# Values of two cycles multiplied together, first memory loads inside the last gate visit, sums of the last head shared with GpSimd

## The chip, the cores and the metric

The kernel runs on one core of a Trainium2 chip. The metric is the device time of one execution in microseconds, the median of several runs. Matrix products run on TensorE (PE; its weight loads are listed as PEld), the other engines are VectorE (DVE), ScalarE (ACT) and GpSimd (POOL); SyncE (SP) issues the DMAs. The times "granted clock 1.0" and "0.5" stand for TensorE at 2.4 and at 1.2 GHz.

## The reference: what is computed

One step of a hybrid encoder layer on 2048 prompt positions and 8 x 16 sample positions, width 1024. One input projection gives queries, keys, values, gates and state inputs. Three mixers run side by side and an output projection joins them:

```python
    fq, fk, fv, fg, ff, su, sg, mq, mg = split_columns(h @ w_in)
    fox_out = fox_attend(fq, fk, fv, logf).reshape(B, T, FOX_WIDTH) * jax.nn.silu(fg)
    ssm_out = ssm_y * jax.nn.silu(sg)
    mem_out = memory_attention(mq, mem_k, mem_v).reshape(B, T, MEM_WIDTH) * jax.nn.silu(mg)
    mix = jnp.concatenate([fox_out, ssm_out, mem_out], axis=-1) @ w_out
    return x + mix, fk, fv, logf, h_re, h_im
```

The forgetting attention (fox) has 8 heads of 64 channels, causal; the memory attention (mem) has 4 heads of 64 over 256 memory tokens. Both take the softmax of their scores over the keys and multiply it with the values.

## The kernel before

The kernel has three stages. The input projections run until about 789 us: 7 passes (state, keys, values, queries, memkv, memq, gate), each over the 17 position tiles (memkv over its two memory tiles), a tile being a "visit" of three parts. Attention of the prompt runs from there to about 1262 us, and the output projection to the end at 1453 us. All three are written as lists of steps; each engine walks the same list and does the steps that are its own, so the list is each engine's order, and semaphores hold the engines together.

**The attention list** (`attention_order`, L1924). Each of the 8 heads has six units of four query tiles: fox0, fox4, mem0, mem4, fox8, fox12 (fox8 is the fox unit whose first tile is 8). A unit has one "scores" block for each key tile: 4, 8, 2, 2, 12 and 16, which makes 44 a head, 352 in all. Four blocks make a cycle: 11 cycles a head, 88 in all (`CYCLE = 4`). Cycles are counted from 0 here. In one cycle stand, in this order:

- "copied": ACT takes the outputs of the units that ended in the cycle before out of PSUM (L2621)
- "scores": PE, two matmuls a block, L2481 and L2486 (and a mask, L2483); "exp": ACT, L2610, into one of 16 slots of `probs_turned`
- "top": PE makes scores in the other orientation some 20 blocks ahead (L2464, L2468, mask L2471), and DVE takes the maximum of each row (L2812, L2818). With the last top of a unit DVE writes `diag` (L2829)
- "row": PE turns a unit's `diag` into a row (L2475) and ACT copies it next to the queries (L2600). The second matmul of a unit's first score waits for that copy
- "add": the exponentials of a block are added to the unit's sum, on POOL, but blocks 2, 3, 6 and 10 of fox8 and fox12 on DVE; of the last head (head 7) all blocks of fox8 and fox12 on DVE (L2780, L2782). "both" (DVE, L2838) joins the two sums; it waits for POOL's part
- "den": two cycles after a unit has ended PE turns its sum (L2494) and DVE adds it up (L2844) and inverts it (L2848)
- "values": PE multiplies exponentials and values (L2512), two tiles of 64 output columns side by side
- in head 7 from its second cycle on: "w_split" (ACT, L2628) and "w_low" (POOL, L2735) split two rows blocks of the output weights, "t_split" (ACT, L2640) and "t_low_early" (POOL, L2739) split sums of them, "gated" (POOL, L2706) multiplies the sample tile by its gates. "mix" (PE, L2535) turns that tile and needs "gated". The pair list ends with the first products of the output projection ("product", PE, L2580), "first_sum" and "y" (DVE, L2892, L2929)

**The PSUM ring** (`Ring`): scores, tops, rows and dens take six banks in turn. PE may fill a bank when the step that used it before has been read: a score by ACT's exp, a top or a den by DVE, a row by ACT.

**The seam between the stages.** The first 12 tops and row 0 are three "hooks" ("attention" steps 0 to 2), laid after the three parts of the last gate visit (`beside[NV - 1, n]`, L373). The steps "first" (DVE L1561) and "second" (DVE L1587, then SP's store L735) of a visit finish a tile's gates; those of the last visit stand behind the visit. Two things wait for them: the sixth bank of the ring, and the first "values". The loads of head 0's values and memory keys (`load_values(sp, 0)`, 8 DMAs, L2242) stand at the start of SP's attention program, and so behind the store of the last gate tile. The tops 12 to 15 (mem0, mem4; L2464), in the first cycle, wait for these loads.

## Time and profile before

| | us |
|---|---|
| median of 3 runs | 1453.31 (1453.03 to 1454.95) |
| profiled execution | 1454.54 |
| its span | 1452.8 |
| busy: PE / DVE / ACT / POOL | 1397.1 / 976.3 / 610.5 / 553.5 |

The span is the time between the first and the last instruction of the trace; 1.7 us lie around it. PE is busy for 96% of it, so the profile is read from PE: first how long it stood and for whom, then at which clock it ran, then what lies between its matmuls. Busy sums count overlapping matmuls once, and a matmul's own length (0.40 us) is longer than the distance at which such matmuls start (0.24 us).

### The profile page before, as it was taken

The page shows a single profiled execution, that of the slowest core. Times are in us where ns is not written, and L with a number is a line of the kernel's source. Part 1 is how long each engine was busy: PE and PEld are TensorE (multiplying, and loading weights), DVE is VectorE, ACT ScalarE, POOL GpSimd, SP SyncE. Part 2 cuts the span into 40 slices and gives each one's busy share as a digit, 9 for nine tenths or more (in the row PEclk, how much of TensorE's full clock was granted, in tenths as well). Part 3 has the DMA queues.
Part 4 walks back from the last instruction along what each step waited for, and adds up shares of the span by engine and source line. Part 5 has one row for each costly group of instructions (what it writes and reads, how often), then busy time and mean ns, then how long its engine had stood idle before and what let it go on. Part 6 is the DMA issues. An engine that isn't in the chain of part 4 may idle for free.

```text
span 1452.8 us, 24958 instructions
## 1 busy us (share of the span) xinstructions
PE 1397.1 (96%) x8510; PEld 1105.9 (76%) x8510; DVE 976.3 (67%) x1827; ACT 610.5 (42%) x1220; POOL 553.5 (38%) x580
## 2 busy tenths in 40 slices
PE   8999999999999989999998899999999999899998
PEld 8999767788877767777776677777777777578886
DVE  4789754782566787655334577787786767987774
ACT  6766422432434363435332344444444445431221
POOL 1121433100043252112003366776776658534442
PEclk9999999999999999999999899999999999899999
DMA  7884799986279587788983935726627432446552
GB/s 226 305 285 174 249 235 254 317 258 193 84 181 350 162 263 254 256 276 275 329 274 103 259 74 113 149 49 128 133 51 153 93 62 66 140 161 200 185 186 89
DMA packets 207565, 275.82 MB, mean 190 GB/s; under 512 B 49424, under 2 KB 146096, under 8 KB 203952
## 3 DMA queue, kind: packets, MB, share of 16 engines
q1 hardware_dynamic: 206400, 274.22, 64.9%
q8 instruction: 70, 1.15, 0.3%
q14 instruction: 55, 0.45, 0.1%
q10 hardware_dynamic: 1040, 0.00, 0.0%
HBM read 186.93 MB, written 86.00 MB: 188 GB/s over the span
## 4 chain that ended last, share of the span: by engine, by line
PE 55%; DVE 7%; issue 3%; DMA 2%; SPq 2%; ACT 2%; POOL 1%; DVEq 0%; ACTq 0%; POOLq 0%
PE in_g L925 13%; PE attn_pv L2512 8%; PE attn_s L2580 6%; PE attn_s L2481 5%; PE attn_pv L2580 5%; PE attn_s L2486 4%; PE attn_s L2468 4%; DVE attn_acc_v L2782 2%; DVE attn_tops L2818 2%; PE in_b L1100 1%; DMA in_xu<-scratch_xt 1%; DVE attn_den L2844 1%; POOL in_hv L1808 1%; PE attn_s L2475 1%; PE attn_s L2494 1%
## 5 line engine op out<-in xcount | busy, mean ns | idle before, releaser
L925 PE MATMUL in_g<-in_wh,in_xh 128*128 128x512 f32 (+2 forms) x904 | 331.4, 380 | 5.4 <-DVE in_wl L1519 1.9
L925 PE MATMUL in_g<-in_wl,in_xh 128*128 128x512 f32 (+2 forms) x904 | 321.9, 369 | 0.0
L925 PE MATMUL in_g<-in_wh,in_xl 128*128 128x512 f32 (+2 forms) x904 | 235.0, 379 | 1.4 <-DVE in_xl L1530 1.3
L2782 POOL TENSOR_TENSOR attn_probs<-attn_probs,attn_probs_turned 128x512 f32<-128x512 f32 (+3 forms) x184 | 196.4, 1067 | 86.9 <-ACT attn_probs_turned L2610 65.6
L2610 ACT ACTIVATE attn_probs_turned<-attn_s 128x512 f32<-128x512 f32 (+1 forms) x352 | 161.5, 544 | 155.9 <-PE attn_s L2486 155.9
L2818 DVE TENSOR_REDUCE attn_tops<-attn_s 128x1 f32<-128x512 f32 (+3 forms) x288 | 159.7, 617 | 94.0 <-PE attn_s L2468 71.5
L925 PEld LDWEIGHTS in_g<-in_wh,in_xh 128*128 128x128 f32 x904 | 165.5, 189 | 39.7 <-issue 6.3
L925 PEld LDWEIGHTS in_g<-in_wl,in_xh 128*128 128x128 f32 x904 | 165.6, 189 | 28.0
L925 PEld LDWEIGHTS in_g<-in_wh,in_xl 128*128 128x128 f32 x904 | 158.0, 189 | 34.8 <-issue 5.2
L1806 POOL TENSOR_SCALAR in_hs<-in_hs 128x8 f32<-128x8 f32 (+1 forms) x53 | 19.7, 372 | 401.8 <-DVE in_hs L1557 401.8
L2512 PE MATMUL attn_pv<-attn_probs_turned,attn_v 128*64 128x256 f32 (+1 forms) x1216 | 146.3, 371 | 0.0
L2512 PEld LDWEIGHTS attn_pv<-attn_probs_turned,attn_v 128*64 128x64 f32 x1216 | 86.9, 140 | 48.4 <-issue 20.2
L1217 ACT ACTIVATE in_xh<-in_xu 128x512 fp32r<-128x512 f32 x174 | 99.6, 623 | 49.0 <-DMA in_xu<-scratch_xt 49.0
L1530 DVE TENSOR_TENSOR in_xl<-in_xu,in_xh 128x512 fp32r<-128x512 f32 x106 | 68.7, 689 | 32.8 <-ACT in_xh L1217 32.3
L1808 POOL TENSOR_TENSOR in_hv<-in_hs,all_neghalf 128x8 f32<-128x8 f32 (+1 forms) x53 | 84.0, 1585 | 4.4
L2780 POOL TENSOR_TENSOR attn_probs<-attn_probs_turned 128x512 f32<-128x512 f32 x38 | 50.3, 1332 | 59.0 <-ACT attn_probs_turned L2610 59.0
L1258 ACT ACTIVATE in_x_turned<-in_tr 128x512 fp32r<-128x512 f32 (+1 forms) x53 | 27.5, 520 | 88.8 <-PE in_tr L947 79.9
L2481 PE MATMUL attn_s<-all_x,all_y 128*128 128x512 f32 (+3 forms) x160 | 62.3, 390 | 1.9 <-DVE in_stage L1587 1.9
L2481 PE MATMUL attn_s<-attn_qa,attn_ka 128*128 128x512 f32 (+3 forms) x160 | 62.2, 389 | 1.7 <-DVE attn_den L2844 1.7
L2486 PE MATMUL attn_s<-all_x,all_y 97*128 97x512 f32 (+3 forms) x160 | 61.3, 383 | 0.5 <-ACT all_x L2600 0.5
L2486 PE MATMUL attn_s<-attn_qb,attn_kb 97*128 97x512 f32 (+3 forms) x160 | 61.2, 383 | 0.0
L1577 DVE TENSOR_TENSOR in_work<-in_g,in_hr 128x512 f32<-128x512 f32 (+1 forms) x53 | 31.4, 592 | 37.9 <-POOL in_hr L1811 37.0
(380 smaller groups left out, 2756.2 us busy)
## 6 DMA issues: line engine op xcount, KB each, us to landing
in_xu<-scratch_xt SPq DMA_DIRECT2D x87, 512.0 KB, 5.3
in_xl<-scratch_xt SPq DMA_DIRECT2D x34, 512.0 KB, 4.5
in_raw<-in_w_in SPq DMA_DIRECT2D x40, 256.0 KB, 5.4
scratch_xt<-in_xu SPq DMA_DIRECT2D x19, 512.0 KB, 4.5
scratch_xt<-in_xl SPq DMA_DIRECT2D x17, 512.0 KB, 5.0
scratch_k<-in_x_turned SPq DMA_DIRECT2D x17, 512.0 KB, 7.2
scratch_q<-in_x_turned SPq DMA_DIRECT2D x17, 512.0 KB, 5.4
in_x_turned<-in_x_prompt SPq DMA_DIRECT2D x16, 512.0 KB, 4.9
```

Source lines behind the costliest of these rows:

```text
L925: last = X.matmul(g_ps[b][:, 0:m], x, ws[:, c, w0:w0 + m], start=(c == 0 and h == 0 and ws is wh), stop=(c == KC - 1 and h == 1))
L1217: F(xh[:, item_visit[j] % 2, 4 * h:4 * h + 4, :], xu[:, j % 2, 4 * h:4 * h + 4, :], ACT.Copy)\
L1530: V.tensor_tensor(xl[:, v % 3, 4 * h:4 * h + 4, :], xu[:, j % 2, 4 * h:4 * h + 4, :], fl(xh[:, v % 2, 4 * h:4 * h + 4, :]), ALU.subtract). ...
L1808: G.tensor_tensor(hv[:, 0:m], hs[:, 0:m], K.neghalf[:, 0:m], ALU.pow).then_inc(s_hchain, 1)
L2468: last = X.matmul(bank[:, at:at + n, :], qb[h][0:LANE, q], kb[h][0:LANE, keys], start=True, stop=not masked)
L2481: X.matmul(bank[:, part:, :], y2[h][:, keys], x2[h][:, q], start=True, stop=False)
L2486: X.matmul(bank[:, part:, :], y1[h][0:FULL, keys], x1[h][0:FULL, q], start=False, stop=True)\
L2512: last = X.matmul(v_ps[u.n % 2][lane * HD:(lane + 1) * HD, tiles[0] // 2:EACH // 2, :], vals[:, k, :], pt[:, s % SLOTS, tiles[0]::2, :], s ...
L2580: last = X.matmul(y_ps[at], ms[left][:, c, :], ws, start=(begins and c == 0 and k == 0), stop=(ends and c == HALF - 1 and k == 2))
L2610: F(pt[:, s % SLOTS, at:, :], ring_ps[ring.at["scores", s]][:, at:, :], ACT.Exp).then_inc(s_exp, 1)
L2782: E.tensor_tensor(acc[:, part:, :], acc[:, part:, :], mine, ALU.add).then_inc(added[engine], 1)
L2818: V.tensor_reduce(top_parts[:, joined[u.n] % 2, i, k // 4:k // 4 + 1], bank[:, 0:n, :].rearrange("p n k -> p (n k)"), AX.X, ALU.max).then_ ...
```

## The change

1. `TOGETHER = 2`: the "values" of an even and the following odd cycle now stand together at the end of the odd one, sorted by unit, each unit's "copied" right behind its last values. "den" steps stand in odd cycles only, ahead of the values, for units that ended two or more cycles earlier.
2. `load_values(sp, 0)` and the waits ahead of it move out of SP's attention program into `sync_begin`, which SP runs at hook 0.
3. The hooks move by one part: hook 0 after part 1, hook 1 after part 2, hook 2 (with row 0) behind "first" and "second" of the last visit.
4. In head 7 fox8's sums are shared as in other heads: 4 blocks on DVE, 8 on POOL, and a "both". fox12's stay on DVE.
5. "t_split" and "t_low_early" 0 and 1 stand one cycle earlier, ahead of "gated" 0. Product (0, 1) stands ahead of the last "den".

```diff
-    for n in range(HOOKS):
-        beside[NV - 1, n] = [("attention", n)]
-    order = projection_order(items, visits, behind, beside)
+    for n in range(HOOKS - 1):
+        beside[NV - 1, n + 1] = [("attention", n)]
+    order = projection_order(items, visits, behind, beside) + [("attention", HOOKS - 1)]
...
+                if what == "attention" and n[0] == 0:
+                    K.begin[0](sp)
...
-            late = u.head == FOX_HEADS - 1 and u.first >= 8
+            late = u.head == FOX_HEADS - 1 and u.blocks > 12
...
-        if c - 1 in ended:
-            order += [("copied", u) for u in ended[c - 1]]
...
-        if c - 2 in ended:
-            order += [("den", u) for u in ended[c - 2]]
-        order += [("values", b) for b in mine]
         ended[c] = [n for n in range(len(units)) if CYCLE * c < score_end[n + 1] <= CYCLE * (c + 1)]
         order += [("both", n) for n in ended[c]]
+        waiting += mine
+        if c % TOGETHER == TOGETHER - 1 or c == cycles - 1:
+            order += [("den", n) for e in range(c) if e + 2 <= c for n in ended[e] if ("den", n) not in order]
+            for n in sorted({scores[b][0].n for b in waiting}):
+                order += [("values", b) for b in waiting if scores[b][0].n == n]
+                if score_end[n + 1] <= waiting[-1] + 1:
+                    order.append(("copied", n))
+            waiting = []
...
+        if n in (KC, KC + 1):
+            order += [("t_split", n - KC), ("t_low_early", n - KC)]
         if n == KC + 1:
             order.append(("gated", 0))
-        if n in (KC + 1, KC + 2):
-            order += [("t_split", n - KC - 1), ("t_low_early", n - KC - 1)]
...
-    order += [("copied", n) for n in ended[cycles - 1]]
-    order += [("product", 0, 0)] + [("den", n) for n in ended[cycles - 1]]
-    order += [("product", 0, 1), ("first_sum", 0), ("t_split", 2), ("t_split", 3), ("mix", 1)]
+    order += [("product", 0, 0), ("product", 0, 1)] + [("den", n) for n in ended[cycles - 1]]
+    order += [("first_sum", 0), ("t_split", 2), ("t_split", 3), ("mix", 1)]
...
-        def sync_program(sp):
+        def sync_begin(sp):
             sp.wait_ge(K.s_cleared, 1)
...
+        def sync_program(sp):
             sp.wait_ge(*K.end_products)
```

The order of SP at the seam, before (`in_stage` are gate tiles that are stored, `attn_v` to `attn_mv` the 8 loads):

```order
L861 DMA scratch_mwide<-in_late 64x128
L735 DMA scratch_fox_gate<-in_stage 128x512 x4
L2242 DMA attn_v<-out_fox_v_prompt 128x16x64
L2242 DMA attn_mqa<-scratch_mq 64x1024 x2
L2242 DMA attn_mqb<-scratch_mq 64x1024
```

And now:

```order
L863 DMA scratch_mwide<-in_late 64x128
L737 DMA scratch_fox_gate<-in_stage 128x512 x3
L2246 DMA attn_v<-out_fox_v_prompt 128x16x64
L2246 DMA attn_mqa<-scratch_mq 64x1024 x2
L2246 DMA attn_mqb<-scratch_mq 64x1024
L2246 DMA attn_mka<-scratch_mk 64x256 x2
L2246 DMA attn_mkb<-scratch_mk 64x256
L2246 DMA attn_mv<-out_mem_v_prompt 128x2x64
L737 DMA scratch_fox_gate<-in_stage 128x512
```

The 8 loads have passed the store of the last gate tile.

The order of PE where the first cycles meet, before (L2464 are the mem tops, L2475 row 1, L2512 the values of cycle 0, L2481 and L2486 the scores of cycle 1):

```order
L2464 MATMUL attn_s<-attn_mkb,attn_mqb 128x256 x8
L2468 MATMUL attn_s<-all_y,all_x 128x512 x2
L2475 MATMUL attn_s<-attn_diag,attn_onesr 128x512
L2512 MATMUL attn_pv<-attn_probs_turned,attn_v 64x256 x2
L2512 MATMUL attn_pv<-attn_probs_turned,attn_v 64x128
L2512 MATMUL attn_pv<-attn_probs_turned,attn_v 64x256
L2512 MATMUL attn_pv<-attn_probs_turned,attn_v 64x128 x3
L2481 MATMUL attn_s<-all_x,all_y 128x512
L2486 MATMUL attn_s<-all_x,all_y 128x512
```

And now, where the lines stand five further down (L2480 is row 1, L2486 and L2491 are the scores):

```order
L2469 MATMUL attn_s<-attn_mkb,attn_mqb 128x256 x8
L2473 MATMUL attn_s<-all_y,all_x 128x512 x2
L2480 MATMUL attn_s<-attn_diag,attn_onesr 128x512
L2486 MATMUL attn_s<-all_x,all_y 128x512
L2491 MATMUL attn_s<-all_x,all_y 128x512
```

The scores of cycle 1 stand directly behind row 1, and the values of both cycles behind the tops and rows of cycle 1.

The order of POOL in head 7 from its fifth cycle on, before (L2735 "w_low", L2706 "gated" 0, L2739 "t_low_early"):

```order
L2780 TENSOR_TENSOR attn_probs<-attn_probs_turned 128x512 x2
L2735 TENSOR_TENSOR attn_w_lo<-attn_w_raw,all_y 128x1024 x2
L2735 TENSOR_TENSOR attn_w_lo<-attn_w_raw,all_x 128x1024 x2
L2735 TENSOR_TENSOR attn_w_lo<-attn_w_raw,all_y 128x1024 x2
L2706 TENSOR_TENSOR attn_out<-attn_out 128x512
L2706 TENSOR_TENSOR attn_out<-attn_out 128x256
L2739 TENSOR_TENSOR attn_t_lo<-attn_t_raw,attn_t_hi 128x1024 x2
```

And now (L2785 and L2787 are adds, L2740 "w_low", L2744 "t_low_early", L2711 "gated" 0):

```order
L2785 TENSOR_TENSOR attn_probs<-attn_probs_turned 128x512
L2740 TENSOR_TENSOR attn_w_lo<-attn_w_raw,all_y 128x1024
L2787 TENSOR_TENSOR attn_probs<-attn_probs,attn_probs_turned 128x512 x3
L2740 TENSOR_TENSOR attn_w_lo<-attn_w_raw,all_x 128x1024
L2787 TENSOR_TENSOR attn_probs<-attn_probs,attn_probs_turned 128x512
L2787 TENSOR_TENSOR attn_probs<-attn_probs,attn_probs_turned 128x384
L2787 TENSOR_TENSOR attn_probs<-attn_probs,attn_probs_turned 128x128
L2740 TENSOR_TENSOR attn_w_lo<-attn_w_raw,all_x 128x1024
L2740 TENSOR_TENSOR attn_w_lo<-attn_w_raw,all_y 128x1024 x2
L2744 TENSOR_TENSOR attn_t_lo<-attn_t_raw,attn_t_hi 128x1024 x2
L2711 TENSOR_TENSOR attn_out<-attn_out 128x512
L2711 TENSOR_TENSOR attn_out<-attn_out 128x256
```

Seven adds have come in, and "gated" 0 stands behind both "t_low_early".

## Rows read from the trace of the kernel before

**Rows 1.** The page, busy time of TensorE: us, share of the span, instructions.
```profile
PE 1397.1 (96%) x8510; PEld 1105.9 (76%) x8510; DVE 976.3 (67%) x1827; ACT 610.5 (42%) x1220; POOL 553.5 (38%) x580
```
**Rows 2.** Busy us by stretch: PE, PEld, DVE, ACT, POOL, then granted clock, DMA.
```profile
804.80:811.80 7.00, 6.94 (x27) 5.23 (x28) 5.07 (x8) 0.97 (x2) 0.00 (x0) 0.50 1.01 207
...
812.00:1228.00 416.00, 413.88 (x2693) 310.60 (x2693) 307.24 (x537) 196.01 (x422) 280.41 (x245) 1.00 0.50 109
...
1269.00:1272.70 3.70, 3.70 (x12) 3.02 (x13) 2.06 (x4) 0.00 (x0) 0.30 (x1) 0.54 1.04 373
```
**Rows 3.** Who PE waited for from 740 us: total us, times, longest.
```profile
PE attn_s L2464 <- DMA attn_mv<-out_mem_v_prompt: 9.9, 1, 9.9
PE attn_s L2494 <- DVE attn_acc_v L2782: 3.5, 1, 3.5
PE attn_s L2468 <- DVE attn_den L2844: 3.3, 7, 2.1
...
PE attn_pv L2580 <- DVE attn_probs L2929: 1.7, 1, 1.7
```
**Rows 4.** Timeline at the seam: start us, us, engine, line, [idle before <- releaser].
```profile
794.53 0.39 SPq L2242 DMA_DIRECT2D attn_v<-out_fox_v_prompt  x1
...
781.90 0.75 DVE L1561 TENSOR_SCALAR in_work<-in_g,in_half 128x512 f32<-128x512 f32 x1 [4.09 <-ACT in_work L1240]
...
793.28 0.69 DVE L1587 SCALAR_TENSOR_TENSOR in_stage<-in_work 128x512 f32<-128x512 f32 x1
...
794.03 0.39 PE L2481 MATMUL attn_s<-all_x,all_y 128*128 128x256 f32 x1 [1.94 <-DVE in_stage L1587]
...
804.86 2.04 PE L2464 MATMUL attn_s<-attn_mkb,attn_mqb 66*128 66x256 f32 x8 [9.92 <-DMA attn_mv<-out_mem_v_prompt]
```
**Rows 5.** Timeline of PE around the values of one cycle, in short windows.
```profile
1000.69 0.49 PE L2494 MATMUL attn_s<-all_ident,attn_probs 128*128 128x128 f32 x3
...
1001.11 1.95 PE L2512 MATMUL attn_pv<-attn_probs_turned,attn_v 128*64 128x256 f32 x16
...
1001.81 0.60 PE L2512 MATMUL attn_pv<-attn_probs_turned,attn_v 128*64 128x256 f32 x4
...
1002.67 0.39 PE L2512 MATMUL attn_pv<-attn_probs_turned,attn_v 128*64 128x256 f32 x2
1002.99 0.50 PE L2481 MATMUL attn_s<-attn_qa,attn_ka 128*128 128x512 f32 x1
1003.32 0.40 PE L2486 MATMUL attn_s<-attn_qb,attn_kb 97*128 97x512 f32 x1
1003.56 0.40 PE L2481 MATMUL attn_s<-attn_qa,attn_ka 128*128 128x512 f32 x1
```
**Rows 6.** Timeline of DVE after the tops of that cycle, and of a row.
```profile
1005.41 2.48 DVE L2818 TENSOR_REDUCE attn_tops<-attn_s 128x1 f32<-128x512 f32 x4 [1.56 <-PE attn_s L2468]
...
1008.13 0.97 DVE L2829 TENSOR_TENSOR attn_diag<-all_ident,attn_negmax 128x512 fp32r<-128x512 f32 x1
...
1012.08 0.45 PE L2475 MATMUL attn_s<-attn_diag,attn_onesr 128*128 128x512 f32 x1
...
1012.56 0.59 ACT L2600 ACTIVATE attn_qb<-attn_s 1x512 fp32r<-1x512 f32 x1 [1.44 <-PE attn_s L2475]
```
**Rows 7.** Last head: POOL, DVE and PE by time, and POOL's adds as a group.
```profile
1225.82 4.75 POOL L2735 TENSOR_TENSOR attn_w_lo<-attn_w_raw,all_y 128x1024 fp32r<-128x1024 f32 x2
...
1250.26 2.89 POOL L2735 TENSOR_TENSOR attn_w_lo<-attn_w_raw,all_y 128x1024 fp32r<-128x1024 f32 x1 [1.52 <-ACT all_y L2628]
1253.11 2.86 POOL L2706 TENSOR_TENSOR attn_out<-attn_out 128x512 f32<-128x512 f32 x2
...
1246.36 10.15 DVE L2782 TENSOR_TENSOR attn_acc_v<-attn_acc_v,attn_probs_turned 128x512 f32<-128x512 f32 x6
...
1258.39 0.96 PE L2535 MATMUL attn_s<-all_ident,attn_out 128*128 128x128 f32 x6
...
L2782 POOL TENSOR_TENSOR attn_probs<-attn_probs,attn_probs_turned 128x512 f32<-128x512 f32 (+3 forms) x184 | 196.4, 1067 | 86.9 <-ACT attn_probs_turned L2610 65.6
```

6 lines of the change are left out of this document (3 added, 3 removed).

## The prediction

> **What bounds the kernel now.** I read the page first: TensorE is busy for 1397.1 of 1452.8 us [rows 1], so a gain must come from PE's standing, its clock, or what lies between its matmuls. The second view is who PE waited for. Behind the seam these waits are few and large: 9.9 us for the loads of head 0, 3.5 us for the last sum, 3.3 us for a den's reading (2.1 of it once), 1.7 us at a product [rows 3]. The third view, the busy time by stretch, shows that two of them cost twice: after the 9.9 us PE worked 7.0 us at a granted clock of 0.50, and after the 3.5 us 3.7 us at 0.54 [rows 2]. Between 812 and 1228 us PE is busy for 413.88 of 416 us, with DVE at 307 and POOL at 280 [rows 2]: only what lies between the matmuls is to be had there. Fourth, the timeline shows what does: the values and their neighbours [rows 5].
>
> **The seam (edits 2 and 3).** The first of the 8 loads was issued at 794.53, and the mem tops, which need all 8, started at 804.86: 10.3 us [rows 4]. What held the loads was the store of the last gate tile, whose data DVE finished at 793.28 + 0.69. SP now only has the store of the tile before ahead of them. Its DVE steps start at 781.90 with L1561 (0.75), then L1587 (0.69, as in the last tile), which no longer has hook 0 in between: 783.4. With the store's issue (0.39, as a load's) the loads start at about 783.8 and are there at 794.1. The other condition is DVE, which reads the twelve early tops and does the last tile's steps in another order but with the same work, and was done at 793.97. The last tile's two steps now stand ahead of hook 2's tops, so the wait of 1.94 us for them [rows 4] turns into a wait for those tops. I take 794.2 for the mem tops: 10.7 us earlier.
>
> In addition PE did 6.94 us of work at half the clock after its long wait [rows 2]; at full clock that is 3.5 us less. A wait of about 3 us remains ahead of 794, after which the clock may still be low, but then PE waits for DVE anyway. **Seam: -14.2 us**, bounds -9 (the loads land 2 us later and the clock stays low for the whole of PE's 7 us) and -16 (PE waits for nothing else behind them).
>
> **Switches between values and the rest (edit 1).** In [rows 5] pairs of value matmuls start 0.215 us apart (1001.81 to 1002.67, four pairs). A transpose has 128 columns where a pair has 256, so 0.11 us; the third of the row starts at 1000.69 + 0.22, and the values at 1001.11, 0.20 later where 0.11 is due: 0.09. From 1001.11 to 1001.81 three pairs take 0.70 for 0.645: 0.05. From the last pair to the scores 0.32 for 0.215: 0.10. Between the first two score matmuls 0.33 for 0.24: 0.09. Together 0.33 us for each visit to the values. There were 88, now there are 44. As a small edge stays where tops now meet scores, I take 0.30: 44 x 0.30 = **-13.2 us**, bounds -9 and -14.5.
>
> **What the values covered.** They lay between the tops of one cycle and the scores of the next, 1.88 us. Now an even cycle's tops are directly followed by scores, and four prices are due.
> (a) A row in an even cycle whose unit starts in the next. fox12's row stands one cycle ahead of its scores; for heads 0, 2, 4 and 6 that is an even cycle. From the row's matmul to the end of ACT's copy 1.07 us pass (1012.08 to 1012.56 + 0.59) [rows 6], of which PE fills 0.47 with the row and one score matmul: 0.65 us, four times, 2.6 us.
> (b) A row in an odd cycle whose last top was read in the even one. Counted from the pair's first score (1002.99), DVE starts on the tops at 2.4, ends at 4.9, and `diag` is there at 6.1 [rows 6]; PE reaches the row after 2 x 1.97 (scores) + 2 x 0.95 (tops) = 5.8. About 20 rows are of that kind: 0.15 each, 3 us; if adds are ahead of DVE, 0.5 each.
> (c) The first three pairs have 12, 10 and 10 tops. Twelve readings at 0.62 us (2.48 for four) [rows 6] and three `diag` are 10 us for DVE, in the stretch in which PE has 7.5 us of scores and tops: 2.5 us, and 1.5 us for the other two.
> (d) The fourth top of an even cycle is read at 4.9 and its bank wanted at 5.1. So DVE must be ready when tops come. Its work in a pair: 5.0 for tops, 0.9 for each add, both or den, 1.1 for a `diag`: 6 to 8 us, but 10.5 in the pairs with three dens, of the pair's 10.8. A late start of some tenths in these: 2 us in all; nothing at best, 12 at worst (0.3 in each pair).
> Sum of the waits: 2.6 + 3 + 4 + 2 = 11.6; **+11.6 us**, bounds +4 and +25.
>
> **The last head (edits 4 and 5).** DVE has 7 adds less and one "both" more there; from 1228 on it was never idle, and the waits of 2.1, 1.7 and 3.5 us for it should go. But POOL takes its place. It worked without a pause up to 1230.57 (1225.82 + 4.75) [rows 7], at "w_low" 3. From there now follow, ahead of "gated" 0: one pair add (1.3), 3 adds (3.4), w_low (2.4), 3 adds (2.6, two are narrow), 3 w_low (7.9), 2 t_low_early (5.3; nearest row: w_low 2.89, same width) and gated 2.86: 25.8 us, to 1256.4, by 1.07 us an add and 2.4 to 2.9 for a split. "mix" 0 stood at 1258.39 and needs it [rows 7]. PE, freed of its waits, would be there at about 1250, so it waits some 4 to 6 us for POOL, and the gain up to mix 0 is 2.0 us. Behind it PE has the values of two cycles (3.6) where it had one at a low clock (2.83): product 0 starts 1.6 us earlier than before. On from there, product (0, 1) covers the last sum (2.8 of the 3.5 us), but "first_sum" now comes after it, and product (0, 2) waits 1.8 us for that (den 0.9, two sums 1.4). The product that waited 1.7 us waits for a chain of DVE steps behind the same den, which begins 3 us earlier: 4.6 us gained in all. Half clocks after the two new waits give back about 2.7. 1.6 + 4.6 - 2.7: **-3.5 us**, bounds -11 (POOL keeps up) and +4 (DVE and POOL hold each other).
>
> Here a rule of the Trainium skill speaks against edit 4. First the row: six adds of DVE took 10.15 us while POOL ran [rows 7], 1.69 each. The rule ("SBUF — State Buffer", section "Who interferes with whom"): a DVE instruction with two SBUF inputs and a GpSimd one that reads SBUF exclude each other, and the later blocks for the whole instruction. My sum has 1.0 us an add for the 15 adds of fox12; by the rule POOL is never idle beside them now, and they take what the row shows.
>
> **Sum.** -14.2 - 13.2 + 11.6 - 3.5 = -19.3 us on the profiled execution's 1454.5: 1435.2. The median of the runs lies 1.2 us below that execution: 1434.0 us.
>
> **The rivals.**
> - *The cover was not needed* (chance 0.20). DVE was busy for 307 of 416 us [rows 2], POOL less; if (b), (c) and (d) cost 4 us instead of 9, and POOL reaches "gated" in time, 5 + 6 more is gained: 1423. Against it: readings come in bursts.
> - *DVE's adds at 1.69 us* (0.13). 15 x 0.69 = 10.4 us more for DVE behind the last both; it has some 6 us in hand before PE wants the last sum. The last den comes 4 us later: 1438. The rule above is this mechanism. Against it: POOL's 12 steps there can each hold up one add at most, and some will meet DVE's other steps.
> - *Half the gain is lost in bursts* (0.16). The waits are 25 instead of 11.6: 1447. For it: (d), since a late DVE shifts both top groups of a pair.
> - *Nothing gained* (0.04): 1451 to 1456, if also the loads run slower beside the last gate products.
> - *Slower* (0.05). DVE misses the second top group in every pair: its adds now stand between two top groups 2.95 us apart, of which the reading takes 2.5. The gains outside are 30.9 us, so it decides from 0.70 us a pair on; at 1.0 us, 44 us are lost: 1467. Against it: the bank of the first top is wanted 0.8 us after it is read, and the values of a pair (3.6 us) let DVE catch up each time.
>
> **How the numbers follow.** The forecast at 1434 has 0.42. Left out are the slower case, "nothing gained" and the outer half of the first and third rival: the range is 1421 to 1448. A measurement of this kernel tells 0.2% (2.9 us) from no change: faster 0.91, within 0.04, slower 0.05.
>
> **What would show it.** Right: the 9.9 us wait is gone and the mem tops start near 794; 44 groups of values of 3.6 us; the clock at 1.0 from about 800 on; PE's waits in the middle are many and under 0.7 us, for ACT's row copy and DVE's `diag` and tops; a wait of 3 to 6 us at mix 0 for POOL's gated; product (0, 2) waits for first_sum. Wrong: waits over 1 us in most pairs, or a clock at 0.5 in the middle, or values that start no closer to each other than before.

## The result: slower, where a gain of 19 us was forecast

| | median us | from, to | runs |
|---|---|---|---|
| before | 1454.13 | 1453.03, 1455.73 | 4 |
| changed | 1460.82 | 1459.53, 1461.62 | 4 |

The ratio is 1.0045, with a 95% interval of 1.0029 to 1.0060. The forecast was 1434.0 us, with a range of 1421 to 1448. Of all runs below one is left out of its comparison, a run of before_den_first of 1937.7 us at a mean granted clock of 0.66. The profiled execution of the changed kernel took 1461.6 us, its span is 1459.9 us, 7.1 more than before. TensorE's busy time is 2.7 us more, so most of the 7.1 are standing:

```profile
PE 1399.8 (96%) x8510; PEld 1120.1 (77%) x8510; DVE 980.8 (67%) x1820; ACT 611.0 (42%) x1220; POOL 569.2 (39%) x587
```

The second view is the busy time by stretch, in the columns of [rows 2]. The stretches are cut at the same pieces of work in both kernels: start of the mem tops, first scores of cycle 2, first scores of cycle 78, first product matmul, its 61st matmul. First the kernel before:

```profile
804.90:817.10 12.20, 12.20 (x59) 8.75 (x59) 8.17 (x14) 4.11 (x8) 3.58 (x3) 0.72 1.02 213
817.10:1208.30 391.20, 389.08 (x2537) 292.09 (x2535) 291.94 (x509) 178.88 (x387) 259.31 (x230) 1.00 0.50 109
...
1208.30:1262.40 54.10, 50.03 (x306) 35.38 (x305) 44.63 (x61) 33.58 (x68) 36.00 (x21) 0.94 0.25 68
1262.40:1285.50 23.10, 17.89 (x76) 13.81 (x76) 16.82 (x22) 5.03 (x9) 8.23 (x7) 0.93 0.71 235
```

and then the changed kernel:

```profile
793.40:808.00 14.60, 14.35 (x60) 10.63 (x60) 8.56 (x15) 4.79 (x10) 6.70 (x6) 0.58 1.03 209
...
808.00:1212.10 404.10, 389.57 (x2536) 302.11 (x2535) 300.87 (x509) 179.61 (x387) 265.47 (x230) 0.98 0.47 103
...
1212.10:1274.50 62.40, 51.34 (x306) 37.64 (x305) 44.26 (x57) 33.17 (x68) 48.63 (x31) 0.89 0.33 94
1274.50:1292.50 18.00, 16.13 (x77) 12.84 (x77) 10.33 (x17) 5.04 (x8) 3.49 (x4) 1.00 0.63 208
```

The changed kernel is 9.1 us ahead when cycle 2 starts, loses 12.9 from there to cycle 78 (the "middle" below), loses 8.3 to the first product, gains 5.1 behind it, and is level after that: -9.1 + 12.9 + 8.3 - 5.1 = +7.0.

**The seam** went as drawn up to the mem tops. In the timeline of the changed kernel (SP, then PE) the first load is issued at 783.06 and the mem tops start at 793.40, 11.5 us earlier than in [rows 4]:

```profile
783.06 0.39 SPq L2246 DMA_DIRECT2D attn_v<-out_fox_v_prompt  x1
...
793.40 2.02 PE L2469 MATMUL attn_s<-attn_mkb,attn_mqb 66*128 66x256 f32 x8
...
797.37 0.79 PE L2491 MATMUL attn_s<-all_x,all_y 97*128 97x512 f32 x1 [0.25 <-ACT all_x L2605]
```

But the granted clock was 0.50, its lower level of 1.2 GHz, from 792.0 to 805.7, so 12.3 us of what follows the mem tops ran at half speed, where before it was 7.0 [rows 2]. In the kernel before the clock was low for longer, from 794.6 to 811.8, but PE stood for all but 0.34 of the first 10.2 us of it; now work runs in that time. From the mem tops to cycle 2 the changed kernel takes 2.4 us more.

**The waits of PE** from 808 to 1212 us, whom it waited for, total, times and longest:

```profile
PE attn_s L2480 <- DVE attn_diag L2834: 4.0, 8, 0.9
PE attn_s L2473 <- DVE attn_den L2849: 3.3, 4, 1.1
PE attn_s L2499 <- DVE attn_negmax L2817: 2.7, 3, 0.9
PE attn_s L2486 <- DVE attn_negmax L2817: 1.9, 3, 0.6
PE attn_s L2491 <- ACT all_x L2605: 1.8, 4, 0.4
PE attn_s L2473 <- DVE attn_tops L2823: 0.8, 1, 0.8
```

They sum to 14.5 us; before it was 2.0 in the same stretch (1.1 and 0.9 for denominators' banks). L2480 is the row, L2473 the tops, L2499 the transposes of a denominator, L2486 and L2491 the scores. **And the clock fell** four times in the middle, where before it never did. Two of the four, each with the stretch ahead of it:

```profile
891.00:897.80 6.80, 5.66 (x40) 3.82 (x37) 6.59 (x9) 2.45 (x5) 6.64 (x5) 1.00 0.01 2
897.80:901.20 3.40, 3.40 (x10) 2.72 (x10) 2.02 (x5) 1.62 (x3) 1.05 (x2) 0.50 0.41 154
...
966.00:972.90 6.90, 5.83 (x42) 4.32 (x39) 6.79 (x12) 1.86 (x5) 6.28 (x5) 1.00 0.29 69
972.90:979.70 6.80, 6.80 (x32) 5.38 (x33) 3.77 (x6) 2.38 (x6) 4.19 (x6) 0.50 1.04 211
```

PE had stood for 1.1 us of the stretch ahead of each of these two falls, for 1.1 of the 10.5 us ahead of the third, and for 0.7 of the 7.0 us ahead of the fourth. That does not tell when the clock falls, though. Here is another stretch of the same kernel, which ends with a wait of 1.08 us for a denominator's bank at 1090.19; the clock behind it stayed at 1.00:

```profile
1083.00:1090.20 7.20, 6.12 (x50) 4.17 (x48) 7.10 (x10) 1.98 (x5) 6.63 (x5) 1.00 0.03 8
```

The four low stretches (897.8, 972.9, 1010.5 and 1147.0) are 17.0 us long, and half of that, 8.5 us, is lost. The middle then reads: waits +12.5, clock +8.5, and -8.1 that is left over: +12.9. The -8.1 is a remainder, taken here for what the switches saved; no run measures it by itself.

One of these waits, in the timeline of PE and of DVE around 971 us:

```profile
969.72 0.45 PE L2473 MATMUL attn_s<-attn_kb,attn_qb 66*128 66x512 f32 x1
971.24 0.56 PE L2473 MATMUL attn_s<-attn_kb,attn_qb 66*128 66x512 f32 x2 [1.07 <-DVE attn_den L2849]
...
968.20 0.69 DVE L2834 TENSOR_TENSOR attn_diag<-all_ident,attn_negmax 128x512 fp32r<-128x512 f32 x1
968.80 1.78 DVE L2787 TENSOR_TENSOR attn_acc_v<-attn_acc_v,attn_probs_turned 128x512 f32<-128x512 f32 x1
970.51 0.68 DVE L2849 TENSOR_REDUCE attn_den<-attn_s 128x4 f32<-128x512 f32 x1
```

The second top block wants the bank that holds the transposed sums of a denominator. The reduction that empties it takes 0.68 us, but stands on DVE behind an addition, and that addition takes 1.78 us where it takes 0.69 alone.

**The last head.** PE waits 3.85 us ahead of the first of the last twelve score blocks, runs at half clock behind that, and then waits 5.11 us for GpSimd's gate (PE, then DVE, then POOL):

```profile
1250.00 0.79 PE L2486 MATMUL attn_s<-attn_qa,attn_ka 128*128 128x512 f32 x1 [3.85 <-DVE attn_den L2849]
...
1267.89 1.54 PE L2540 MATMUL attn_s<-all_ident,attn_out 128*128 128x128 f32 x6 [5.11 <-POOL attn_out L2711]
...
1246.52 2.82 DVE L2843 TENSOR_TENSOR attn_acc_v<-attn_acc_v,attn_probs 128x512 f32<-128x512 f32 x1 [2.93 <-POOL attn_probs L2787]
1249.26 0.68 DVE L2849 TENSOR_REDUCE attn_den<-attn_s 128x4 f32<-128x512 f32 x1
1249.97 0.18 DVE L2853 RECIPROCAL attn_rmem<-attn_den 128x4 f32<-128x4 f32 x1
...
1252.21 6.65 DVE L2787 TENSOR_TENSOR attn_acc_v<-attn_acc_v,attn_probs_turned 128x512 f32<-128x512 f32 x6
...
1255.52 2.79 POOL L2740 TENSOR_TENSOR attn_w_lo<-attn_w_raw,all_y 128x1024 fp32r<-128x1024 f32 x1 [3.96 <-ACT all_y L2633]
...
1262.82 2.66 POOL L2744 TENSOR_TENSOR attn_t_lo<-attn_t_raw,attn_t_hi 128x1024 fp32r<-128x1024 f32 x1 [1.68 <-ACT attn_t_hi L2645]
1265.44 2.39 POOL L2711 TENSOR_TENSOR attn_out<-attn_out 128x512 f32<-128x512 f32 x2
```

The denominator whose bank is wanted at 1250.00 is a memory unit's (its inverse goes to `attn_rmem`). Its reduction stood on DVE behind the new "both" of fox8 (L2843), and that waited 2.93 us for GpSimd's part of the sum and then took 2.82 us itself. So this wait comes of edits 1 and 4 together: in merge_only and in tail_only, which have one of them each, and in after_den_first, where the reduction stands ahead of the "both", no such wait is in the traces. The three waits for DVE that stood here before (2.1, 1.7 and 3.5 us [rows 3]) are all gone.

### The profile page after: what moved, and what is told of

It reads as the page before. It is cut to its first block, busy times and chain, and to the rows that moved or that the text cites. A ratio compares the mean times of both kernels' runs of the same rounds, so it can differ in the third digit from the quotient of the medians.

```text
span 1459.9 us, 24959 instructions
## 1 busy us (share of the span) xinstructions
PE 1399.8 (96%) x8510; PEld 1120.1 (77%) x8510; DVE 980.8 (67%) x1820; ACT 611.0 (42%) x1220; POOL 569.2 (39%) x587
## 4 chain that ended last, share of the span: by engine, by line
PE 53%; DVE 6%; issue 5%; POOL 3%; ACT 2%; DMA 2%; SPq 1%; DVEq 0%; ACTq 0%; POOLq 0%
PE in_g L927 13%; PE attn_pv L2517 9%; PE attn_s L2585 6%; PE attn_pv L2585 5%; PE attn_s L2486 4%; PE attn_s L2491 4%; PE attn_s L2473 4%; DVE attn_tops L2823 1%; PE in_b L1102 1%; PE attn_s L2499 1%; DMA in_xu<-scratch_xt 1%; POOL in_hv L1810 1%; DVE attn_negmax L2817 1%; POOL attn_probs L2787 1%; PE attn_s L2480 1%
## 5 line engine op out<-in xcount | busy, mean ns | idle before, releaser
L2787 POOL TENSOR_TENSOR attn_probs<-attn_probs,attn_probs_turned 128x512 f32<-128x512 f32 (+3 forms) x190 | 213.1, 1122 | 97.7 <-ACT attn_probs_turned L2615 74.5
L2517 PE MATMUL attn_pv<-attn_probs_turned,attn_v 128*64 128x256 f32 (+1 forms) x1216 | 141.1, 375 | 0.0
L2517 PEld LDWEIGHTS attn_pv<-attn_probs_turned,attn_v 128*64 128x64 f32 x1216 | 93.0, 143 | 43.4 <-issue 13.8
L2486 PE MATMUL attn_s<-attn_qa,attn_ka 128*128 128x512 f32 (+3 forms) x160 | 62.8, 392 | 5.8 <-DVE attn_den L2849 3.9
L2785 POOL TENSOR_TENSOR attn_probs<-attn_probs_turned 128x512 f32<-128x512 f32 x39 | 50.1, 1294 | 45.1 <-ACT attn_probs_turned L2615 44.9
L2491 PE MATMUL attn_s<-all_x,all_y 97*128 97x512 f32 (+3 forms) x160 | 63.0, 394 | 2.0 <-ACT all_x L2605 2.0
L2491 PE MATMUL attn_s<-attn_qb,attn_kb 97*128 97x512 f32 (+3 forms) x160 | 63.4, 396 | 0.0
L2486 PE MATMUL attn_s<-all_x,all_y 128*128 128x512 f32 (+3 forms) x160 | 61.9, 387 | 1.5 <-DVE attn_tops L2823 1.5
```

Of the source, the lines that this page charges most:

```text
L2486: X.matmul(bank[:, part:, :], y2[h][:, keys], x2[h][:, q], start=True, stop=False)
L2491: X.matmul(bank[:, part:, :], y1[h][0:FULL, keys], x1[h][0:FULL, q], start=False, stop=True)\
L2517: last = X.matmul(v_ps[u.n % 2][lane * HD:(lane + 1) * HD, tiles[0] // 2:EACH // 2, :], vals[:, k, :], pt[:, s % SLOTS, tiles[0]::2, :], s ...
L2787: E.tensor_tensor(acc[:, part:, :], acc[:, part:, :], mine, ALU.add).then_inc(added[engine], 1)
```

## Experiments: each part alone

Four kernels: the merging alone (edit 1), the seam alone (2 and 3), the last head alone (4 and 5), and all but the merging.

```
merge_only          CYCLE, TOGETHER = 4, 2;   seam and last head as before
seam_only           CYCLE, TOGETHER = 4, 1;   last head as before
tail_only           CYCLE, TOGETHER = 4, 1;   seam as before
seam_tail_no_merge  CYCLE, TOGETHER = 4, 1
```

Expected of merge_only:

> The kernel before with edit 1 alone: the values of two cycles together, the seam and the last head as they were. Theory A (the new short waits of TensorE behind tops, rows and dens cost their own length and also take its clock down): between the scores of cycle 2 and those of cycle 78 some 390 us become 400 to 406, with about 15 us of waits where there were 2, four or five stretches of 3.4 us at the low clock where there was none, and 10 to 11 us saved between values and scores; in all 5 to 14 us slower than before. Theory B (the low clock in the middle comes from another edit, such as the changed seam, and the waits alone are paid for by the saved switches): the clock stays at 1.0 between cycle 2 and 78, and the kernel is within 5 us of before.

Of seam_only:

> The kernel before with edits 2 and 3 alone (the loads of head 0 issued at hook 0, the hooks one part later). Both theories: the mem tops start near 793.4 instead of 804.9, PE works the first 13 us of attention at half clock as in the changed kernel, and 7 to 11 us are gained, all of them before the scores of cycle 2; the middle stays as before, without low clock.

Of tail_only:

> The kernel before with edits 4 and 5 alone (fox8 of the last head shared with GpSimd, both early splits ahead of gated 0, product (0, 1) ahead of the last den). Theory A: GpSimd becomes the late one, mix 0 waits for gated 0 by 3 to 6 us, and the last head with the first products is between 3 us faster and 4 us slower than before. Rival (the late gated 0 in the changed kernel came from the merged values, not from these edits): no wait at mix 0 over 1 us, and 5 to 10 us gained.

Of seam_tail_no_merge:

> The changed kernel with the values of each cycle on their own again (edits 2 to 5 without edit 1). Theory A: the sum of the two runs that change the seam and the last head alone, so some 5 to 14 us faster than before; the middle between cycle 2 and 78 as before (391 us). Theory B: about as slow as the changed kernel, or slower.

| kernel | median us | ratio to before, 95% interval | start of cycle 2 against before | middle, us | from cycle 78 on, against before |
|---|---|---|---|---|---|
| before | | | 0 | 391.2 | 0 |
| changed | 1460.8 | 1.0045 (1.0029 to 1.0060) | -9.1 | 404.1 | +3.3 |
| merge_only | 1467.8 | 1.0101 (1.0075 to 1.0128) | -1.8 | 399.4 | +3.7 |
| seam_only | 1448.0 | 0.9961 (0.9948 to 0.9973) | -9.0 | 391.1 | +4.6 |
| tail_only | 1459.8 | 1.0041 (1.0025 to 1.0056) | -3.2 | 391.1 | +6.5 |
| seam_tail_no_merge | 1451.3 | 0.9988 (0.9975 to 1.0000) | -8.1 | 391.2 | +5.3 |

The last three columns are from one profiled execution each. The start of cycle 2 differs between kernels without the seam edit too (0 to -3.2 here, and up to +1.9 in the kernels of the next section), so two or three microseconds in that column, and what follows from it in the whole, is nothing. The middle does not: in all kernels without merging and with DVE's order as before it is 391.1 to 391.2. The rows of merge_only's and seam_only's middle:

```profile
815.30:1214.70 399.40, 383.73 (x2535) 298.32 (x2534) 300.72 (x509) 179.38 (x387) 265.49 (x230) 1.00 0.47 105
```
```profile
808.10:1199.20 391.10, 389.00 (x2536) 292.09 (x2534) 291.89 (x509) 178.88 (x387) 259.57 (x230) 1.00 0.50 109
```

**What follows.** The seam is the only part that gains: 4.9 us, where 7 to 11 were expected, since 4.6 of the 9.0 us ahead are lost again behind cycle 78. Merging costs 14.8 us alone by the medians (10 in the profiled execution, the fastest of the four), where 5 to 14 were expected, and 9.5 beside the other edits (1460.8 against 1451.3). The edits on the last head cost 6.9 us alone, and there neither expectation held: PE did not wait at mix 0, and nothing was gained. Seam and last head together came out at -1.7 us, where -5 to -14 had been expected. In merge_only PE waited 15.7 us in the middle, in the changed kernel 14.5, but the clock fell there for 3.4 us and here for 17.0. Taken one by one from the two traces the waits are the same to 0.05 us, but for two more in merge_only (0.85 and 0.31 us). So the same waits cost 1.7 us more at the clock in one execution and 8.5 in the other. What decides it is not in the waits, and was not found.

## Experiments: what the merged cycles wait for

Two theories. **A**: DVE's additions stand ahead of what PE waits for. **B**: the order asks too soon, since a row follows its tops without values between them, and eight score and eight top blocks in a row must pass through six banks. merge_light leaves most of VectorE's additions out (its denominators of fox8 and fox12 are then not the reference's), before_light is its control, and merge_row_late gives the diagonal more time.

```
merge_light, before_light  (heads 0 to 6, DVE only)
-    E.tensor_tensor(acc[:, part:, :], acc[:, part:, :], mine, ALU.add)
+    E.tensor_tensor(acc[:, part:, 0:8], acc[:, part:, 0:8], mine[:, :, 0:8], ALU.add)
-    (a block's first sum)
+    E.memset(acc, 1.0)
merge_row_late
     order += [("values", b) ...]
+    while rows < len(units) and top_end[rows + 1] <= before:
+        order.append(("row", rows)); rows += 1       # was ahead of the additions
```

Expected of merge_light, before_light and merge_row_late:

> merge_only with most of VectorE's work on the sums of probabilities left out in heads 0 to 6: its first sum of a block is a memset of 1.0, and each later addition takes 8 of 128 columns, so the denominators of fox blocks 8 and 12 are not the reference's. All waits and the order stay. Theory A (the 15 us of new waits from 808 to 1212 us are VectorE being late: its additions stand ahead of the tops, diagonals and denominators that TensorE waits for, and 40 us of the additions lie in that stretch): those waits fall from about 15 us to under 5, and scores of cycle 2 to scores of cycle 78 take 391.2 - 10.6 = about 381 us instead of 399.5 (merge_only) and 391.2 (before); the whole kernel is some 15 us under merge_only, about 1452. Rival B (the waits come of the order itself: a row or a bank is asked for too soon after the score block that fills it, whatever VectorE has to do): the waits keep 10 us or more and the stretch takes 393 or more. Rival C (the clock): low stretches of the clock remain in the middle though the waits are gone.

> The kernel before with the same work of VectorE left out as in merge_light: the control. Before waits only 2.0 us in the stretch from the first cycles to cycle 78, so both theories expect it to take 389 to 391.2 us there; if it gains more, the lighter VectorE also gives something that has nothing to do with merged cycles (the gap between two kinds of block, contention), and this is to be taken off merge_light's gain. The last head keeps its additions, so the whole kernel should be at 1450 to 1454 us.

> merge_only with the row matmul of each unit written behind the eight value blocks of an odd cycle instead of ahead of them, so that VectorE has some 5 us more between the last tops and the row that needs their diagonal. Theory A (VectorE is late by 0.9 us at a time): the waits for the diagonal (5.8 us in 10) go, but VectorE's lateness shows at the next thing asked of it, the banks of tops and denominators and the score blocks that need the row's copy: the middle stretch gains 0 to 4 us of the 8.3. Rival B (the order asks too soon for the row): the middle gains the 5.8 us and the 2.5 us of the copies' waits, and comes to the 391.2 of before or under it.

The middle of merge_light, with its longest wait under it, of before_light, and of merge_row_late with its two longest waits:

```profile
816.80:1210.30 393.50, 382.22 (x2535) 298.13 (x2534) 282.58 (x509) 179.19 (x387) 257.80 (x230) 1.00 0.48 106
...
PE attn_s L2477 <- DVE attn_diag L2838: 5.0, 10, 0.9
```
```profile
814.30:1200.80 386.50, 386.50 (x2537) 291.33 (x2535) 272.57 (x509) 178.87 (x387) 252.80 (x231) 1.00 0.50 111
```
```profile
818.00:1222.30 404.30, 386.49 (x2535) 302.00 (x2533) 298.49 (x509) 181.08 (x389) 266.82 (x230) 0.98 0.47 103
...
PE attn_s L2470 <- DVE attn_den L2846: 6.8, 4, 2.5
PE attn_s L2483 <- DVE attn_den L2846: 4.3, 2, 2.2
```

Medians: 1461.5 us (ratio 1.0051, 1.0033 to 1.0068), 1449.8 (0.9971, 0.9958 to 0.9984), 1470.1 (1.0120, 1.0102 to 1.0139). **Neither theory alone holds.** With light additions merging costs 393.5 against 386.5, 7.0 us of the 8.2 that it costs with full ones, and 11.1 us of waits are left: A falls as the main cause, and the numbers of B came (10 us of waits or more, 393 us or more). With the rows late the diagonal's waits are gone, as B says, but 11.1 us for denominators' banks stand where 4.5 were, the clock fell for 13.6 us instead of 3.4, and the middle is 4.9 us longer: both expectations missed (0 to 4 us gained by A, the 391.2 of before by B). What the later row gives, VectorE's lateness and the clock take back, and more. The control was a miss of its own: 4.7 us gained where 2.2 at most were expected, with 2.0 us of waits in the profile to be had. That pointed at DVE's order.

The next two take both away, one by leaving work out, one with all work done. merge_adds_late holds the additions of an even cycle back until behind the tops and denominators of the odd one, so that DVE adds during the values.

```
merge_adds_late
-    order += [("add", b) for b in mine]              # each cycle, ahead of den
     if c % TOGETHER == TOGETHER - 1 or c == cycles - 1:
         order += [("den", n) ...]
+        order += [("add", b) ...] + [("both", n) ...]   # of both cycles
merge_row_late_light  =  merge_row_late + merge_light
merge_adds_row_late   =  merge_adds_late + merge_row_late
```

> Both measures at once: the rows behind the values of an odd cycle, and VectorE's additions of heads 0 to 6 left out as in merge_light (the fox denominators of blocks 8 and 12 are again not the reference's). Theory A+B (the new waits have two parts that cover each other: the diagonal is asked for too soon after its tops, and VectorE comes late to the banks of denominators): with both taken away the middle stretch (cycle 2 to cycle 78, 391.2 us before, 386.5 with the light VectorE alone) falls to 376 to 380 us, the 10.6 us of switches at last seen. Rival B (the six banks of the score ring: eight score and eight top blocks in a row ask for more than ScalarE and VectorE can empty, whatever stands in the order): waits for negmax, tops and denominators of 6 us or more stay, and the stretch takes 384 us or more.

> merge_only, with the additions of an even cycle held back on VectorE and GpSimd until after the tops and the denominators of the odd cycle, so that in the burst of scores and tops VectorE only empties banks, and adds while TensorE works through the eight value blocks. All work is done. If VectorE's additions in the burst are what makes it late (Theory A), the middle stretch falls from 399.5 us (merge_only) to about merge_light's 393.5 or under it; if it is the chain of four tops, their negmax and the diagonal (B), the waits for the diagonal (5.8 us) stay and it takes 396 or more. ScalarE's exponentials wait for additions 16 blocks back, so additions that come 4 blocks later can cost something too, at most 2 us.

> merge_only with additions and denominators in the order of merge_adds_late and the rows behind the value blocks as in merge_row_late; all work is done. merge_adds_late took 389.8 us from cycle 2 to cycle 78 (391.2 before, 387.1 unmerged with the denominators first) and still waited 7.1 us for diagonals; merge_row_late_light took 387.6 with most additions left out. Theory: the diagonals' waits go, and 387 to 389 us are left, no better than the unmerged kernel with the same VectorE order: merged cycles then give nothing, because what the switches save goes into waits for the six banks. Rival: 383 us or less, and merging pays after all once VectorE's order is right.

The middles, in that order:

```profile
819.00:1206.60 387.60, 379.42 (x2536) 297.38 (x2534) 280.18 (x509) 180.49 (x389) 258.69 (x230) 1.00 0.48 107
```
```profile
818.50:1208.30 389.80, 379.83 (x2535) 297.68 (x2534) 290.10 (x509) 179.40 (x387) 264.85 (x230) 1.00 0.49 107
```
```profile
815.60:1224.80 409.20, 393.83 (x2536) 307.66 (x2534) 290.29 (x509) 181.59 (x389) 264.51 (x230) 0.96 0.47 103
...
PE attn_s L2484 <- DVE attn_tops L2821: 8.8, 6, 2.1
```

Medians 1455.7 (1.0012, 1.0001 to 1.0023), 1457.2 (1.0023, 1.0014 to 1.0032) and 1477.8 (1.0173, 1.0148 to 1.0197). In merge_row_late_light (376 to 380 us expected, or 384 and more) 7.8 us of waits stay, 3.6 of them for the row's copy by ScalarE, and the middle is 1.1 us longer than before_light's: even then merging does not pay. merge_adds_late brings the middle to 389.8 with all work done, 9.6 us under merge_only's and better than expected (393.5), though 4.4 us of waits for diagonals stay (a later expectation names 7.1, which is not the middle's). It is the only merged kernel with all work done whose middle lies under that of the kernel before, by 1.4 us; in all it is 3.3 us slower than before, and in its last head PE waits 7.3 us for VectorE's sums. merge_adds_row_late was a miss on both sides: 387 to 389 or at most 383 had been expected, and it is the slowest of all. With rows late the score block behind a row wants a bank whose tops DVE has not read, up to 2.1 us, and the clock fell for 23.8 us (865.3, 981.4 and 1100.9). Why the two measures, each fair or bearable alone, do this together was not followed further.

## Experiments: the order on VectorE

The control and the 971 us timeline say the same: DVE reduces a denominator behind the additions of its cycle, and the bank is wanted before. One line moved, on DVE alone (PE has no additions):

```
+    order += [("den", n) ...]
     order += [("add", b) for b in mine]
     ...
-    order += [("den", n) ...]
```

> seam_only with one order changed on VectorE alone: the reduction of a denominator is written ahead of the four additions of its cycle instead of behind them. In the last head these additions take 1.7 to 2.3 us each instead of 0.69 because GpSimd works beside them, and the reduction of block 8's denominator stands behind four of them, with the last score block waiting for its bank 4.1 us. Theory: that wait goes, and of the 4.5 us that the tail of seam_only gave back, 2 to 4 return: 1444 to 1446 us. Rival: the sums of block 12 end later by as much, since VectorE waits for the transposes of the denominator, and the wait only moves to the products' bank or the fold (5.3 us now): no difference from 1448.

> The changed kernel with the same order on VectorE. In its middle 3.3 us of waits for the bank of a denominator and 4.4 us between transposes of denominators should shrink by half, in its last head the 3.9 us before the last score block go: 1453 to 1457 us where the changed kernel takes 1460.8. By the rival (what waits for VectorE is the engine's whole load, not the place of the reduction) it stays at 1459 to 1462.

> The kernel before, with the reduction of a denominator ahead of its cycle's additions on VectorE, and nothing else changed. The middle stretch should fall by the 4.0 us of seam_den_first (391.2 to 387.2), because the time between top blocks falls from 15.5 to 10.8 us in all; in the last head the wait of the last score block (1.7 us) and of the tops (2.1 us) should go, so that the whole kernel takes 1446 to 1449 us. Rival (the gain needs the earlier seam as well): 1450 or more.

> A repeat of seam_den_first (1441.4 us, ratio 0.9917). If its gain is 9 us of seam, 4 of the middle and 1 to 2 of the last head, it lies 7 to 9 us under before_den_first in the same runs, at 1438 to 1442.

| kernel | is | median us | ratio, 95% interval | middle |
|---|---|---|---|---|
| before_den_first | before + this | 1450.3 | 0.9975 (0.9963 to 0.9987) | 387.1 |
| seam_den_first | seam_only + this | 1441.4 | 0.9917 (0.9886 to 0.9948) | 387.2 |
| the same again | | 1441.7 | 0.9920 (0.9907 to 0.9933) | 387.1 |
| after_den_first | changed + this | 1451.3 | 0.9985 (0.9973 to 0.9997) | 395.1 |

The middle of seam_den_first, in which PE does not wait at all, and of after_den_first, with its two longest waits:

```profile
807.20:1194.40 387.20, 387.20 (x2537) 291.04 (x2535) 307.47 (x509) 179.29 (x387) 266.19 (x230) 1.00 0.50 110
```
```profile
807.70:1202.80 395.10, 381.68 (x2535) 296.81 (x2534) 301.34 (x509) 179.41 (x387) 266.76 (x230) 1.00 0.48 106
...
PE attn_s L2481 <- DVE attn_diag L2835: 3.9, 8, 0.9
PE attn_s L2500 <- DVE attn_negmax L2818: 2.7, 3, 0.9
```

**seam_den_first beats both kernels**, by 12 us the one before. The order alone gives 4.1 us in the middle; the whole of before_den_first missed its range, 1450.3 where 1446 to 1449 were expected, and in its last head PE now waited 7.4 us for the sums of fox8 and fox12. seam_den_first and after_den_first came out better than expected (1444 to 1446, 1453 to 1457). In after_den_first the 3.3 us of waits for denominators' banks are gone, 13.4 us of other waits stay (tops' banks took 2.3 of it), and the clock held at 1.00: 9 us gained in the middle, of which 8.5 are the clock's. This holds beyond the one execution: the mean clock of its ten runs is 0.989 to 0.993, that of the changed kernel's four 0.984 to 0.987. Four pairs of kernels now differ in the merging alone:

| | merged, middle | not merged, middle | merged, median | not merged, median |
|---|---|---|---|---|
| merge_only, before | 399.4 | 391.2 | 1467.8 | 1453.0 |
| changed, seam_tail_no_merge | 404.1 | 391.2 | 1460.8 | 1451.3 |
| light additions | 393.5 | 386.5 | 1461.5 | 1449.8 |
| denominators first (not merged: seam_tail_den_first, below) | 395.1 | 387.1 | 1451.3 | 1442.8 |

In these four pairs merging costs 7.0 to 12.9 us in the middle and 8.5 to 14.8 us in all. (The medians of a pair are not always of one occasion; the kernel before itself moved between 1453.0 and 1455.0.) With rows or additions moved as well the middle's cost goes from little to much: merge_row_late_light lies 1.1 us above before_light, merge_adds_late 2.7 us above before_den_first (389.8 against 387.1), and merge_adds_row_late 22.1 us above it. No merged kernel was faster than the best unmerged one with the same work.

## Experiments: the last head

seam_block8 gives GpSimd its share of block 8 and does no more beside the seam, seam_gate_late sets the two early halves ahead of the gate and does no more; neither has the third part of edit 5, product (0, 1) ahead of the last "den". seam_late is seam_tail_no_merge once more, and seam_tail_den_first is it with the denominators first.

```
seam_block8     -late = u.head == FOX_HEADS - 1 and u.first >= 8
                +late = u.head == FOX_HEADS - 1 and u.blocks > 12
seam_gate_late  -n == KC + 1: gated 0;  n in (KC + 1, KC + 2): t_split, t_low_early
                +n in (KC, KC + 1): t_split, t_low_early;  n == KC + 1: gated 0
```

> A repeat of seam_tail_no_merge (edits 2 to 5 without the merging) on another occasion, to see how far the end of the last head repeats: if it follows from the order, the same waits (5.7 us for the denominator's bank, 3.8 us at the products) and the same low stretches come again; if it hangs on how additions of VectorE and operations of GpSimd happen to meet, they differ by a microsecond or more.

> seam_only, and of the last head only block 8's sums shared with GpSimd. Theory A (GpSimd's additions of block 8 push its splits of weights together, without the idle 5 to 8 us between them, beside VectorE's additions of block 12, which then take 2.3 us each instead of 1.7): the wait of the last score block for the denominator's bank grows from 4.1 to about 5.7 us, a denominator's wait of 2 to 3 us appears ahead of the tops, and the kernel takes 1450 to 1452 us against 1448.0. Rival B (VectorE has eight additions fewer, so its last ones come sooner): 1444 to 1447. The low stretches of the clock in the last head, 17 us in all in seam_only, can move either by 1 to 2 us.

> seam_only, and of the last head only the two early halves ahead of the gate on GpSimd. The prediction's rival says that the gate comes late for the first transposes and costs 4 to 6 us; in the unmerged kernel GpSimd reaches it some 9 us before the transposes, so no wait is expected there, and 1446 to 1449 us against 1448.0. If it is 1450 or more, this edit is the one that costs, by GpSimd's four splits in a row beside VectorE's additions.

> Edits 2 to 5 (no merging) with the reduction of a denominator ahead of the additions. Against seam_den_first (1441.4 us) it tells what the edits on the last head give when the wait for the denominator's bank is out of the way. There TensorE waited 7.2 us for the sums of block 12, whose additions VectorE starts late because those of block 8 stand ahead of them. Theory A: with a share of block 8 on GpSimd VectorE is through earlier and this wait halves: 1437 to 1440 us. Rival B (the additions collide with GpSimd's splits, as before): 1442 to 1446.

Medians 1450.9 (0.9979, 0.9967 to 0.9991), 1447.0 (0.9956, 0.9938 to 0.9974), 1448.9 (0.9965, 0.9952 to 0.9978) and 1442.8 (0.9923, 0.9899 to 0.9948). From cycle 78 on, against 239.3 us before: seam_late 247.2, seam_block8 244.0, seam_gate_late 244.5, seam_tail_den_first 243.9; seam_only has 243.9, seam_den_first 241.0 and 238.7. So neither of these two alone can be told from seam_only's 1448.0 (expected were 1450 to 1452 or, by the rival, 1444 to 1447 for seam_block8, and 1446 to 1449 for seam_gate_late, which held), while edits 4 and 5 as a whole cost 3 us. Whose these 3 us are stays open: the moved product (0, 1) was never run alone, and in every kernel that has it PE waits 1.6 us at a product for "first_sum", which neither seam_block8 nor seam_gate_late shows. With the denominators first edits 4 and 5 make no difference (1442.8 against 1441.4 and 1441.7, with intervals that overlap); 1437 to 1440 had been expected, or 1442 to 1446 by the rival. The profiled execution of seam_tail_den_first is the slowest of its seven (1450.0), so its 243.9, and its start of cycle 2, are the slow end of that kernel. seam_late repeats the waits of seam_tail_no_merge to a tenth (5.7 and 2.8 us for denominators' banks, 1.6 at a product) but for one at a product (4.7 against 3.8). The waits there belong to the order, not to chance; its other 1.7 us are the clock's, which was low for 17.0 us instead of 13.6.

What the edits meet is in tail_only's timeline (DVE, then POOL):

```profile
1224.89 5.35 DVE L2782 TENSOR_TENSOR attn_acc_v<-attn_probs_turned 128x512 f32<-128x512 f32 x1
...
1244.45 13.70 DVE L2784 TENSOR_TENSOR attn_acc_v<-attn_acc_v,attn_probs_turned 128x512 f32<-128x512 f32 x6
...
1224.82 1.30 POOL L2782 TENSOR_TENSOR attn_probs<-attn_probs_turned 128x512 f32<-128x512 f32 x1
1226.05 2.42 POOL L2737 TENSOR_TENSOR attn_w_lo<-attn_w_raw,all_y 128x1024 fp32r<-128x1024 f32 x1
1228.39 4.38 POOL L2784 TENSOR_TENSOR attn_probs<-attn_probs,attn_probs_turned 128x512 f32<-128x512 f32 x3
```

Six additions take 13.70 us, 2.28 each, where six took 10.15 before [rows 7]: from cycle 78 on DVE is busy for 184.12 us with 243 instructions, where it was 182.50 with 250, so it lost more by the company than it was spared by the additions handed over. In the changed kernel it did not come to that: 177.70 us there, and fox12's 15 additions took 15.8 us, 1.05 each (six of them are the row at 1252.21 above). What stays open is why seam_only, with the same orders there as before, takes 4.6 us more in this stretch, with 12.5 us of waits against 9.2 and 17.0 us of low clock against 10.2: six of its additions take 12.08 us where 10.15 stood before, so they met GpSimd otherwise, but what moved the two against each other was not found.

## Why the prediction was wrong, step by step

Forecast and measured, in the profiled execution:

| stretch | forecast | measured |
|---|---|---|
| seam | -14.2 | -9.1 |
| middle: switches | -11.4 (38 of the 44 pairs) | -8.1, all that the waits and the clock do not explain |
| middle: waits | +11.6 | +12.5 |
| middle: clock | 0 | +8.5 |
| last head | -3.5, and -1.8 for the six other pairs | +3.3 |
| sum | -19.3 | +7.1 |

- **The loads of the seam: right.** Mem tops at 794.2 forecast, 793.40 measured, the wait of 9.9 us gone.
- **The seam's clock: the step that failed there** is "after which the clock may still be low, but then PE waits for DVE anyway". PE waited 0.25 us. The low stretch began 1.4 us ahead of the mem tops and covered 12.3 us of work, not 7.0: the term of -3.5 was +2.4. The bound of -9 was right at the edge: in ten profiles with the seam edit cycle 2 starts between 5.1 and 11.8 us early.
- **The switches**: 0.30 us each was too much as a net gain, the remainder is 0.21. What the waits and the clock leave in the changed kernel, merge_only, merge_light and after_den_first, each against its unmerged fellow, is 5.4 to 8.1 us for 38 pairs, 0.14 to 0.21 us each. Where the rest went, waits of a tenth that the view of waits does not list or smaller savings, the rows do not tell.
- **The waits: right in their sum, roughly in their kinds.** (a) 1.8 us in 4 waits for ScalarE's copy, where 2.6 in 4 stood. (b) 4.0 us for the diagonal, where 3 stood, but in 8 waits of 0.2 to 0.95 us and not in about 20 of 0.15. (c) and (d) together 8.7 for banks (3.3 + 2.7 + 1.9 + 0.8), less the 2.0 of before, where 6 stood; the largest, 3.3 for banks of denominators, stands in none of the four by name. The longest is 1.1 us, where under 0.7 was forecast.
- **The clock in the middle: the term that was missing.** The text named a clock at 0.5 in the middle as a sign of error and gave it no price. With waits of 1.1 us at most 8.5 us were lost to it. By the ends of the sum (+25 for the waits) it was inside the bounds; the likeliest value had no place for it.
- **The last head**: the step that failed is "PE, freed of its waits, would be there at about 1250". The three waits named went, but in their place came 3.85 us behind the new "both", which the sum counted as one more operation of DVE and not as one that waits for GpSimd with a denominator behind it, and 2.1 us for two rows; the clock was at half for 6.8 us from 1249.4. To the first product +8.3 us, where -1.6 stood. PE's wait for the gate (5.1 us, 4 to 6 forecast) has the right size by luck: counted from cycle 78 PE was there 9.0 us later than forecast and GpSimd 7.6 us later, since GpSimd, which was to work without a pause, stood for 5.6 us waiting for ScalarE's splits. Behind the first product 5.1 us were gained (4.6 forecast), and the wait for "first_sum" was 1.6 us (1.8 forecast).
- **The rival "DVE's adds at 1.69 us"** did not come true in the changed kernel: the 15 additions took 1.05 us each, as in the sum (1.0), and PE did not wait for the last sum. Its mechanism shows elsewhere, at 2.28 us in tail_only, and in the 2.82 us of the "both" at 1246.52. The argument against it, that each of GpSimd's steps can hold up one addition at most, bounds little: in the row at 1224.89 one addition took 5.35 us, through three instructions of GpSimd.
- **The rival "half the gain is lost in bursts"** came nearest for the middle: it had 25 us of waits, where waits and clock together were 21.0.
- **The rival "slower"** gave the right direction, but it was not this case: it wanted 1 us in every pair. What made the kernel slower was each term falling short at once: 5.1 at the seam, 12.7 in the middle, 8.6 in the last head.
